# A two-model kernel with another order of splits, tables, compressed attention and the last projection

## The reference

```python
x = layer_even(x, norm0, w_in0, w_out0)      # top-k and dilated attention, heads 0 to 15
x = layer_odd(x, norm1, w_in1, b_f1, w_out1) # stick-breaking and forgetting attention, heads 16 to 31
x = rmsnorm(x, norm_f)
h = x
h = h + 0.5 * rmsnorm_2(swiglu(rmsnorm_2(h, g1), w_gate, w_up, w_down), p1)       # "ff1"
z = rmsnorm_2(h, mix_pre_g) @ w_in                                                 # "mix"
o_attn = nsa_attention(...)   # compressed keys (gelu(blocks @ w1) @ w2), selected and windowed keys
o_rec  = rglru_block(...)     # gated linear recurrence
o = concat(rmsnorm_2(o_attn, g_a), rmsnorm_2(o_rec, g_r))                          # "attn", "rec"
h = h + rmsnorm_2(o @ w_out, mix_post_g)
h = h + 0.5 * rmsnorm_2(swiglu(rmsnorm_2(h, g2), w_gate2, w_up2, w_down2), p2)     # "ff2"
gate = sigmoid(rmsnorm_2(h, ple_pre_g) @ w_ple_gate)
h = h + rmsnorm_2(gate * (p @ w_ple_proj), ple_post_g)                             # "ple"
```

## Time and profile before

| | us |
|---|---|
| median of 3 runs | 2988.22 (2987.42 to 2989.7) |
| the profiled execution | 2986.73 |
| its span on the core | 2984.9 |
| PE busy | 2895.3 (97%) |
| DVE busy | 1728.3 (58%) |
| ACT busy | 1292.6 (43%) |

### The profile page before, as it was taken

How to read it: one execution, slowest core, us unless ns; L and a number is a source line. 1 busy time by engine, 2 the same in 40 slices (tenths; PEclk the granted TensorE clock), 3 DMA queues, 4 the chain that set the end, 5 groups by cost and what they waited for, 6 DMA issues and landing times.

```text
span 2984.9 us, 33278 instructions
## 1 busy us (share of the span) xinstructions
PE 2895.3 (97%) x13556; PEld 2408.0 (81%) x13556; DVE 1728.3 (58%) x1631; ACT 1292.6 (43%) x1336; POOL 12.4 (0%) x16
## 2 busy tenths in 40 slices
PE   8999999999999999999999999998999999999997
PEld 7878788878888788888888788876788888888876
DVE  5469755345555655555555766765655555555574
ACT  5444444444444533333334454544533334333353
POOL 0000000000000000000000000000000000000000
PEclk9999999999999999999999999998999999999999
DMA  7545355544445555565555566532555555555644
GB/s 235 191 154 192 99 184 185 190 163 160 152 142 196 189 193 188 191 191 188 195 185 192 169 184 221 161 107 99 187 192 188 195 185 192 187 195 185 196 167 143
DMA packets 275615, 530.60 MB, mean 178 GB/s; under 512 B 8640, under 2 KB 32336, under 8 KB 274752
## 3 DMA queue, kind: packets, MB, share of 16 engines
q1 hardware_dynamic: 275088, 528.25, 54.2%
q0 software_dynamic: 432, 0.99, 0.1%
HBM read 527.12 MB, written 2.10 MB: 177 GB/s over the span
## 4 chain that ended last, share of the span: by engine, by line
PE 89%; DVE 4%; ACT 3%; issue 2%; DMA 1%; SPq 0%; DVEq 0%; ACTq 0%
PE ps L660 27%; PE ps L662 27%; PE ps L661 27%; ACT w_hi L1260 2%; DVE w_lo L1838 1%; PE ps L678 1%; PE ps L680 1%; PE ps L679 1%; PE ps L740 1%; PE ps L826 1%; DVE work L2063 0%; PE ps L846 0%; DVE st L2078 0%; PE ps L856 0%; PE ps L770 0%
## 5 line engine op out<-in xcount | busy, mean ns | idle before, releaser
L1838 DVE TENSOR_TENSOR w_lo<-raw,w_hi 128x2048 fp32r<-128x2048 f32 (+2 forms) x503 | 1126.7, 2244 | 810.2 <-ACT w_hi L1260 809.3
L1260 ACT ACTIVATE w_hi<-raw 128x2048 fp32r<-128x2048 f32 (+2 forms) x503 | 942.4, 1878 | 1024.6 <-DMA raw<-in_ff_w_down 318.0
L660 PE MATMUL ps<-w_hi,x_hi 128*128 128x512 f32 (+4 forms) x3176 | 1236.2, 389 | 15.4 <-DVE x_lo L1987 8.9
L662 PE MATMUL ps<-w_hi,x_lo 128*128 128x512 f32 (+4 forms) x3176 | 1224.9, 386 | 0.0
L661 PE MATMUL ps<-w_lo,x_hi 128*128 128x512 f32 (+4 forms) x3176 | 1224.5, 386 | 0.0
L660 PEld LDWEIGHTS ps<-w_hi,x_hi 128*128 128x128 f32 x3176 | 599.0, 189 | 135.6 <-DVE x_lo L1987 9.4
L662 PEld LDWEIGHTS ps<-w_hi,x_lo 128*128 128x128 f32 x3176 | 598.9, 189 | 118.4
L661 PEld LDWEIGHTS ps<-w_lo,x_hi 128*128 128x128 f32 x3176 | 599.7, 189 | 114.6
L660 PE MATMUL ps<-w_hi,h_hi 128*128 128x512 f32 x652 | 253.9, 389 | 2.0 <-DVE h_lo L2640 2.0
L662 PE MATMUL ps<-w_hi,h_lo 128*128 128x512 f32 x652 | 253.7, 389 | 0.0
L661 PE MATMUL ps<-w_lo,h_hi 128*128 128x512 f32 x652 | 253.6, 389 | 0.0
(11 more groups left out here) (309 smaller groups left out, 1507.3 us busy)
## 6 DMA issues: line engine op xcount, KB each, us to landing
raw<-in_w_in SPq DMA_DIRECT2D x139, 1024.0 KB, 5.1
raw<-in_ff_w_gate SPq DMA_DIRECT2D x88, 1024.0 KB, 5.2
raw<-in_ff_w_up SPq DMA_DIRECT2D x88, 1024.0 KB, 5.2
raw<-in_ff_w_down SPq DMA_DIRECT2D x88, 1024.0 KB, 5.1
raw<-in_w_out SPq DMA_DIRECT2D x48, 1024.0 KB, 5.1
raw<-in_w_ple_gate SPq DMA_DIRECT2D x16, 1024.0 KB, 5.1
raw<-in_w_in SPq DMA_DIRECT2D x8, 696.0 KB, 4.3
z<-in_rows SPq DMA_DIRECT2D x5, 1024.0 KB, 7.4
```

The source lines that it names most:

```text
L660: nc.tensor.matmul(o, x[0][:, k0 + c, s], hi[:, c, 0:width], start=first and c == 0, stop=False)
L662: m = nc.tensor.matmul(o, x[1][:, k0 + c, s], hi[:, c, 0:width], start=False, stop=last and c == n - 1)
L1260: nc.scalar.activation(landed_part(w_hi, u, j), landed_part(raw, u, j), ACT.Copy).then_inc(hi_ready, 1)
L1838: V.tensor_tensor(landed_part(w_lo, u, j), landed_part(raw, u, j), landed_part(w_hi, u, j).bitcast(F32), ALU.subtract).then_inc(parts_read ...
```

## The change

- **Layer 0's heads.** q and k of head 0 are turned one unit earlier, its logits come before the loop. DVE splits w_lo at even heads right behind the mask (`beside_first_head`) and ahead of the write-out, and drains or gates at odd heads.
- **Layer 1's heads.** q and k of head 16 are turned one unit earlier; at head 17 ACT and DVE split two units further ahead.
- **Tables.** The angle chain, Sin, the softplus of lambda and two halved biases move from the mixer to the first units of layer 1.
- **Norms.** DVE's order in `tiled_first_block` is another: the last drain by tile, then root, update, gain of tile 0 first. PE turns tile 1 in the middle of the unit's tile 0, and tiles 2 and 3 in the middle of its tile 1. At the end of a feed-forward the third split moves: ACT's between the two tail roots, DVE's behind x_lo of tile 1 (mix) or among the steps of ple.
- **Projection.** Block 2 of w_ple_proj is multiplied within ff2's norm, blocks 0 and 1 within ple's, block 3 at the end. ACT copies the three (`kept`). p is loaded after `rec_lo`, turned once in MIX_OUT + 3, and its parts have a place of their own. The gate's drains multiply and weight as they come, and ACT sums their squares.
- **Compressed stage.** The transposes for it come two units earlier (in MIX_REC), the copies on ACT too; cmp_k_w2 and cmp_v_w2 are loaded behind MIX_Y's units, with a semaphore of their own; the second product is a unit later.
- **Mixer's heads.** A loop of its own on each engine: one item per head, ahead of the write-out; 18 half units instead of 16 (`halves_beside` and three more); MIX_Q2's chunks in the order 8, 12, 0, 4; the compressed steps one or two heads earlier; the recurrence's norm as eight operations at head 34 in place of two large ones before the heads.
- **Attention norm.** Four rows are scaled into four buffers; half a unit, the four transposes, half a unit.
- **w_out.** Block 2's second part has four units of two chunks (512 KB) instead of two of four, and block 3 starts with two of two.

The core of the diff:

```diff
-    MIX_Q2 = plan(t["w_in_2"], ZQ + BW, [BW])
+
+    MIX_Q2 = in_turn([(t["w_in_2"], ZQ + BW, BW, quarter((8, 12, 0, 4)))])
 
     OUT_PART = in_turn([(t["w_out_2"], 2 * BW, BW, quarter((8, 12)))])
     MIX_OUT = in_turn([(t["w_out_2"], c * BW, BW, quarter((8, 12, 0, 4))) for c in range(2)], [0, 0, 1, 1, 0, 0, 1, 1])
-    in_turn([(t["w_out_2"], 2 * BW, BW, quarter((0, 4)))])
-    in_turn([(t["w_out_2"], 3 * BW, BW, quarter((8, 12, 0, 4)))])
+
+    in_turn([(t["w_out_2"], 2 * BW, BW, [(k, 2) for k in (0, 2, 4, 6)])])
+    in_turn([(t["w_out_2"], 3 * BW, BW, [(8, 2), (10, 2)] + quarter((12, 0, 4)))])
+
+    PROJ_AT_MIX = plan(t["w_ple_proj_2"], 2 * BW, [BW], 2)
     FF2 = plan_other(12 * FB)
+    PROJ_AT_FF = plan(t["w_ple_proj_2"], 0, [BW] * 2, 2)
     PLE_GATE = plan(t["w_ple_gate_2"], 0, [BW] * 4)
-    PLE_PROJ = plan(t["w_ple_proj_2"], 0, [BW] * 4, 2)
+    PROJ_LAST = plan(t["w_ple_proj_2"], 3 * BW, [BW], 2)
+    KEPT = {PROJ_AT_FF: 0, PROJ_AT_FF + 1: 1, PROJ_AT_MIX: 2}
     N_UNITS = len(block_of)
     first_unit = [b[0] for b in blocks]
     end_unit = [units_of[b][-1] + 1 for b in range(len(blocks))]
@@ -161,8 +167,8 @@
 
     turned_before, gained_before, n_turned, n_gained = {}, {}, 0, 0
...
-        halves_beside = [2, 2, 1, 1, 1, 1, 0, 0] + [1] * 7 + [0]
-        units_ended = [sum(halves_beside[:n + 1]) // 2 - sum(halves_beside[:n]) // 2 for n in range(16)]
+
+        halves_beside = [1, 2] + [1] * 4 + [1] * 7 + [0, 0, 1]
 
...
-            load_units(first_unit[MIX_COMPRESSED], end_unit[CMP[0]] + 4)
+            load_units(first_unit[MIX_COMPRESSED], first_unit[MIX_Y])
 
 
             sp.wait_ge(parts_used, end_unit[CMP[0]])
             for m, name in enumerate(("rg_w_a", "rg_w_i")):
                 sp.dma_start(rg[:, m], t[name].rearrange("b i j -> i b j")).then_inc(mix_landed, 16)
+            load_units(first_unit[MIX_Y], first_unit[MIX_Q])
             for m, name in enumerate(("cmp_k_w2", "cmp_v_w2")):
-                sp.dma_start(cmp_w2[:, m], t[name].rearrange("(k p) n -> p k n", p=P)).then_inc(mix_landed, 16)
-            load_units(end_unit[CMP[0]] + 4, first_unit[OUT_PART])
+                sp.dma_start(cmp_w2[:, m], t[name].rearrange("(k p) n -> p k n", p=P)).then_inc(cmp_landed, 16)
+            load_units(first_unit[MIX_Q], first_unit[OUT_PART])
...
+            load_units(first_unit[OUT_PART], first_unit[MIX_OUT] + 4)
+            sp.wait_ge(made["rec_lo"], 1)
+            sp.dma_start(p_in, t["p"]).then_inc(p_landed, 16)
+            load_units(first_unit[MIX_OUT] + 4, first_unit[FF2])
...
                 turn_tile(0)
-                turn_tile(1)
+                for _ in others:
+                    advance(1, (p_hi, p_lo))
+                if others:
+                    turn_tile(1)
                 for g in range(4):
                     def before(tt):
-                        if tt and g < 3:
+                        if tt and 0 < g < 3:
                             turn_tile(2 * g + 2)
                             turn_tile(2 * g + 3)
                         pe.wait_ge(st_done, turned_before[name] + 2 * g + tt + 1)
 
-                    next_unit(g, before)
+                    def mid(tt):
+                        if tt == 0 and not others:
+                            turn_tile(1)
+                        elif tt:
+                            turn_tile(2)
+                            turn_tile(3)
+
+                    next_unit(g, before, mid if g == 0 else None)
 
             def last_and_first_block(name, src, ready, next_unit):
 
@@ -800,8 +831,8 @@
...
+            def mixer_heads():
+                turn_qk(32)
+                advance_halves(1)
+                logits(32)
+                for n in range(32, 48):
+                    if n + 1 < 48:
+                        if n + 1 in (36, 40):
+                            pe.wait_ge(rotated, 6 if n + 1 == 36 else 7)
+                        turn_qk(n + 1)
+                    advance_halves(halves_beside[n - 32])
+                    if n in (45, 46):
+                        mix_compressed(n - 45)
+                    if n > 32:
+                        mix(n - 1)
+                    if n + 1 < 48:
+                        logits(n + 1)
+                    if n == 44:
+                        turn_compressed()
+                    turn_probs(n)
+                pe.wait_ge(made["cmp_added"], 2)
+                advance_halves(1)
+                mix(47)
+                advance_halves(1)
+
...
+            advance_half(0)
             for s in range(4):
                 turn_attention(s)
-                if s == 1:
-                    pe.wait_ge(st_done, turned_before["attn"] + 2)
-                    advance(1)
+            advance_half(1)
...
+                    if tt == 0:
+                        split_next(at[0] + 1)
...
+                    if n == 17:
+                        split_next(at[0] + PARTS)
+                        split_next(at[0] + PARTS + 1)
+                        held(n, True)
...
+                split_at = (32, 33, 35, 37, 39, 41, 43, 45, 46)
+                u = first_unit[MIX_Q2] + PARTS
...
-            def tiled_first_block(name, update, norm, first, second, third):
-
+            def tiled_first_block(name, update, norm, last, others, first, second, third):
+
+                last(0)
                 tail_rstd(0)
                 update(0, 0)
+                last(1)
+                gain_tile(name, 0, 0)
                 first()
+                if not others:
+                    lo_tile(name, 0, 0)
                 tail_rstd(1)
-                gain_tile(name, 0, 0)
                 update(0, 1)
-                lo_tile(name, 0, 0)
+                if others:
+                    lo_tile(name, 0, 0)
+                second()
                 gain_tile(name, 0, 1)
-                second()
                 lo_tile(name, 0, 1)
                 update(1, 0)
                 update(1, 1)
@@ -2149,38 +2230,33 @@
                         copy_probs(n - 1)
                     stick = jobs[n][4] == "stick"
                     (stick_logits if stick else negate)(n)
...
+        attn_rows = [scaled[:, 0], scaled[:, 1], work[:, 2048:2560], work[:, 2560:3072]]
...
+                elif kind == "tanh" and b < PLE_GATE + 3:
                     dve.wait_ge(drained[pair_of[b]], drains_before[b] + 1)
+                    j = b - PLE_GATE
+                    c = slice(j * BW, (j + 1) * BW)
+                    V.scalar_tensor_tensor(out2[:, :, c], place_of(b), 1.0, last_weighted[j], ALU.add,
+                                           ALU.mult).then_inc(made["ple_gated"], 1)
+                    dve.wait_ge(made["ple_gated"], j + 1)
                     dve.wait_ge(grow_landed, 80)
-                    j = b - PLE_PROJ
-                    V.tensor_tensor(last_weighted[j], place_of(b), gain_row(j),
-                                    ALU.mult)
+                    V.tensor_tensor(last_weighted[j], out2[:, :, c], gain_row(j), ALU.mult)
...
-            until(first_unit[MIX_TOGETHER])
+            until(first_unit[MIX_REC] + 2)
             pe.wait_ge(st_done, turned_before["mix"] + 8)
-            pe.wait_ge(rotated, 3)
+            pe.wait_ge(rotated, 4)
...
+            def beside_first_head(n):
+
+                if n % 2 == 0:
+                    if n:
+                        split_next(at[0] + PARTS)
+                    return
+                if n > 1:
+                    finish_unit()
+                if n == 7:
+                    gate_heads(0, 0)
+                elif n == 11:
+                    gate_heads(0, 1)
+                elif n == 13:
+                    y_lo(0, 0)
+
...
+                split_at = (33, 35, 36, 39, 40, 42, 46)
+                u = first_unit[MIX_Q2] + PARTS
+                for n in range(32, 48):
+                    if n > 32:
+                        copy_probs(n - 1)
+                    negate(n)
+                    if n in split_at:
+                        split_next(u)
+                        u += 1
+                    if n == 32:
+                        turn_heads(ZKS, 2, True)
+                    elif n == 34:
+                        normed_recurrence()
+                    elif n == 37:
+                        dve.wait_ge(made["rec_hi"], 1)
+                        V.tensor_tensor(x_lo[:, LB:2 * LB, :], by_block(r1), x_hi[:, LB:2 * LB, :].bitcast(F32),
+                                        ALU.subtract).then_inc(made["rec_lo"], 1)
+                    elif n == 38:
+                        all_drained(dve, OUT_PART)
+                        turn_heads(ZQ + BW, 4, True)
+                    elif n == 43:
+                        compressed_logits()
+                    elif n == 44:
+                        compressed_probs()
+                    elif n == 45:
+                        compressed_added(0, 40)
+                    elif n == 47:
+                        compressed_added(1, 44)
+                    if n > 32:
```

(10 more changed lines are left out.)

481 lines of the change are left out of this document (251 added, 230 removed).

## The result

The changed kernel takes 2921.11 us, median of 4 runs (2916.88 to 2922.12), against 2987.98 of the kernel before (4 runs): a ratio of 0.9775, interval 0.9763 to 0.9787. That is 66.9 us less. The direction and most terms were right, and the gain was 15 us larger than forecast.

What follows compares the result with a forecast made beforehand. PE was taken as the bound, with only its idle time, half clock and the ends to win. Stage terms summed to 53.2 us, less 2 for joints 51.2, giving 2936 us, range 2923 to 2956.

Steps and rivals of the forecast that it cites:

- the first sum: Whole kernel: span 2984.9 less PE's busy 2895.3 gives 89.6 us idle, divided over the stages by their windows.
- Layer 0's heads: Layer 0's heads: split put into DVE's wait and head 0 turned early; 0.6 of 5.5 us idle stay, +4.9.
- The mixer's heads and the attention norm: Mixer: DVE's wait filled with one item per head, +12; four attention rows scaled into four buffers, +13.5.
- joints between stages: Between stages, where halves now meet: 2 us taken off the sum of 53.2.
- The compressed stage: Compressed stage: ACT's queue gap of 6.7, SP load gaps of 2.4 and two half-clock stretches go, +12.5 (4 to 14).
- The mixer's norm: Mixer's norm: DVE's split delays the second group, −1.7, and 1.8 more for ACT behind it: −3.5 (−5 to +2).
- ff2's norm: ff2's norm: one projection block, 2.7 us, fills gaps of 4.0 and a half-clock stretch: +1.6 (0 to 3).
- (a): Mixer's heads and norms: DVE becomes the bound, 10 + 5 us of gain lost, 2951; chance 0.15.
- (b): Compressed stage: stays bound by its loads, 10 us stay, 2946; chance 0.08.
- (c): Norms: their new order wins after all, the two losses of 7.5 us are zero, 2928; chance 0.10.
- (d): Layer 0's and mixer's heads: split before write_out stands on every head's chain, slower, 3034; chance 0.03.
- the low end: Whole kernel: forecast with upper bounds for mixer's norm +5, heads +3, attention +1.5, ple +3: 2923.

Runs made afterwards that it cites:

- after_5: The changed kernel run again with no further change, beside the kernel with the mixer's split moved: 2920.39 us (5 runs).

## Why the prediction was right or wrong

**What bounds the kernel.** Right in kind: the gain came from PE's stalls and half clock, and DVE's and ACT's work stayed the same.

**The step that failed is the first sum.** "Idle is 2984.9 − 2895.3 = 89.6 us", and each stage's idle was taken from its window as what its stalls cost. A matmul's row of 512 columns is 0.16 us longer than the distance to the next, so each stall behind one costs that much more than shown, and short ones do not show. Layer 0's heads were forecast at +4.9 on 5.5 idle; they gave 9.1. The idle term was right (5.5 to 0.6); 4.2 us were hidden in the "busy" time. In the mixer's heads, undoing DVE's order alone showed 3.2 of 12.1 hidden.

**The mixer's heads and the attention norm.** 25.5 forecast, 32.7 measured. The count of distances divides it: idle time went from 22.5 to 0.7, 21.8 us; the stretches at half clock had cost some 7.6, and some 3.3 were hidden. So 3.3 of the missing 7.2 us are the first sum again, and the other 3.9 are the allowance for what would stay. The forecast left 4.3 us in the heads, 2.5 to 4 of them for items that exceed their slot, and 1.7 at the attention norm; 0.7 were left. Against that it counted the gap of 1.5 us at 2031 twice, since the 10.8 us of the attention norm's window already hold it. Why nothing stayed is not shown. The slack of a head was read from one wait of DVE (1.95 us), but PE's half units between the turned probabilities and the product may cover a late copy too, and two halves more were put in; no run took these back alone.

**The other terms that missed.** The 2 us taken off for joints between stages had no row behind them, and no such loss was measured. The +1.3 of the start is no part of the sum.

**The compressed stage.** 14.0 against 12.5. The mechanism was half right: the SP load is worth 4.8 us, 2.9 of them gaps and the rest a clock stretch, near what was worked out (2.4 and a stretch). Of the 6.7 us the place of the transposes made 5, not ACT's queue. One of the 14.0 lies behind the stretch that the forecast read.

**Right in size.** The tail at +12.6; layer 1 at 5.9 for 5.3; w_out at −2.3 for −1.7, with its gap of 1.48 us where a long unit is issued three short ones ahead.

**Right in size, in part by luck.** The mixer's norm at −3.5. The second unit starts 1.8 us later against the rest, for a forecast of 1.7, behind DVE's split, which moving the split confirmed. But the further 1.8 "for ACT behind it" was the clock: the stretch now stands behind that start instead of ahead of it, and in the 13 us from there PE makes 58 matmuls instead of 67 with no idle time. And the gaps ahead of the transposes went, but 2.44 and 0.78 us came ahead of the products of tile 0 and tile 1, which the forecast does not have. Ple's norm has −4.9 for −4.0 with a half-clock stretch in the first trace; in the next two traces of the same kernel it did not come, and the stage cost 3.4.

**ff2's norm.** −0.2, not +1.6, in the first trace, with the half-clock stretch that was forecast to go. In `after_5` the stretch did not come and the stage gave +1.4. So the term was sized right, and took for certain what the clock does in some runs only.

**The rivals.** (a), DVE as the bound, did not happen: DVE is busy for 77 of 97 us in the heads and PE idle for 0.7. (b): no load is waited for in the compressed stage. (c) was wrong too, for the norms lost what was forecast; its time, 2928, was nearest only since the heads gave more. (d) did not happen: the two stages with the early items won 9.1 and 32.7 us.

**The range.** The 2 us taken off for joints and the low end were built from the terms' own idle. A bound for what idle hides, 0.16 us for each of the 57 places in layer 0's heads, is up to 9 us there alone; with it the range would have held the time, which lies 2 us outside.

## What to carry to other kernels

Read a stall of PE from start to start against the usual distance, not from the idle time of its row; where there are many short stalls, count the places and multiply. Work beside a head's chain belongs in the wait of its engine; here it paid too to keep a unit's split and another's drain in different heads. Where a split and a chain share DVE, look for its idle time ahead of the chain before you give the split a place inside it.

## What the runs showed of the chip

The same gap of PE, in the same stage, is followed by a half-clock stretch of 3.4 us in some runs and not in others. Counted over the traces of the changed kernel and its variants that have the gap:

| gap of PE | where | followed by half clock |
|---|---|---|
| 1.37 us | at 852.9 | 8 of 17 traces |
| 1.8 us | ff2's norm | 11 of 15 |
| 2.2 us | ple's norm | 4 of 15 |
| 2.5 us | at 956 | 5 of 17 |
| 2.96 us | the mixer's norm | 14 of 14 |

After gaps of 1.4 to 2.5 us the cost of the clock, 1.5 us, is here a chance, and the length of the gap alone does not give it: the two of 2.2 and 2.5 us were followed by it less often than those of 1.37 and 1.8. I had counted it as certain wherever the trace of before had it. What decides it no run here shows.
